# Paged decode attention: score tiles spread over eight 32x32 tiles, page turns moved further ahead, and the scores split round the values

## Chip, core and metric

The kernel runs on one core of one Trainium2 chip. The metric is the device time of one execution in microseconds (us): the median of three runs.

## What is computed

One inference step of a two-layer hybrid model, for a prompt of 1024 tokens and eight sample sequences of one new token each. The change touches one part alone: the attention of the eight new tokens of layer 0 over a paged cache of 8192 past positions (64 pages of 128 positions for each sequence). Everything is float32. Cut to what matters:

```python
past_ckv = cache_mla_ckv[li][page_table].reshape(n, -1, 256)      # n = 8 sequences, 8192 positions
past_kr  = cache_mla_krope[li][page_table].reshape(n, -1, 32)
q_lat  = einsum('nthd,chd->nthc', q_nope, w_uk)                   # 16 heads
s_past = (einsum('nthc,nlc->nhtl', q_lat, past_ckv) + einsum('nthr,nlr->nhtl', q_rope, past_kr)) * scale
p      = softmax(concat([s_past, s_new]))
o_lat  = einsum('nhtl,nlc->nthc', p[..., :l], past_ckv) + ...
```

## The kernel before, in words

The decode loop walks over 32 units (`WU`): eight sequences times four units of 16 pages (`UP`). A page is 128 positions x 288 numbers (256 latent and 32 rotary), 144 KB. For each unit w:

- **Fetch.** 16 DMAs bring the pages into one of three slots of `ck` (`CKS`), positions on partitions. For each of the four groups of four pages, SP issues two pages (`fetch_sp`, line 1176) and ACT issues the other two (`fetch_act`, line 1182). A slot may be refilled once the values of the unit that used it are done (`pv_done`). The issuing line is 1171.
- **Turn.** VectorE (DVE) transposes each group of four pages in 32x32 blocks from `ck` into one of two slots of `ckT` (`turn`, line 1308; the instruction is line 1311, 128x1152). In `ckT` the partition quarter b (partitions 32b to 32b+31, `quads[b]`) holds 32 columns of the cache for the positions of quarter b of each page.
- **Scores.** TensorE (PE) multiplies in 32x32 tiles (`scores`, line 1218; the instruction is line 1228). The nine steps j cover the 288 columns. In each step quarter b of `ckT` goes through the tile at row quarter b and column quarter b, so four tiles of the array's sixteen work at a time. One half of a unit is eight pages, that is 256 score columns. Both halves go into one PSUM bank, `x = w % 2`.
- **Softmax.** DVE takes the running maximum (`maximum`, line 1339: reduce at 1344, small copies across quarters to 1355), ACT takes the exponential (lines 1289 and 1291), DVE turns the probabilities (`turn_prob`, line 1357, instruction 1359), PE multiplies with the pages (`values`, line 1233, instruction 1241: all 128 rows, one column quarter for each page group) and DVE adds to the sums (`outputs`, line 1361, instructions 1366 and 1368).

Each engine has its instructions in an order written by hand, and they meet through semaphores. PE's order is: for each w, the second half of scores(w), the first half of scores(w+1), values(w). DVE's order for each w is: turn groups 0 and 1 of w+1, outputs(w-1), maximum(w), turn group 2 of w+1, turn_prob(w), turn group 3 of w+1. ACT's order for each w is: the exponentials of w, then the eight page issues of unit w+2. SP issues its pages one unit after another, waiting only for `pv_done`. While DVE does maximum(w), PE works on the first half of scores(w+1), whose groups 0 and 1 are turned already.

A float32 matmul stands in the trace as two records, so 72 matmuls of a unit's scores are 144 records, and the 16 of its values are 32.

Of the kernel before, what the change touches and what calls it, by code (L numbers as in the profile page):

```python
# [142 lines left out]
def build(nc, A, O):  # L143
    with ExitStack() as outer:
# [995 lines left out]
        with ExitStack() as ctx:  # L1140
# [38 lines left out]
                for g in range(4):  # L1179
                    fetch(sp, mybir.EngineType.SP, w, g, sp_pages)  # L1180

            def fetch_act(act, w):
                if w >= CKS:
                    act.wait_ge(pv_done, w - CKS + 1)
                for g in range(4):
                    fetch(act, mybir.EngineType.Activation, w, g, act_pages)

            with nc.Block() as block:
# [7 lines left out]
                @block.tensor  # L1196
                def _(pe):
                    MM = nc.tensor.matmul
                    pe.wait_ge(dec_w_in, 48)
                    for h in range(H):  # L1200
                        for c in range(2):
                            m = MM(bank[:, 6, (c * H + h) * NS:(c * H + h + 1) * NS], wukT[:, h, c * P:(c + 1) * P],
                                   qs[0:NOPE, h, :], start=True, stop=True)
                    m.then_inc(pe_i, 1)
                    pe.wait_ge(dve_i, 1)
                    for n in range(NS):
                        for half in range(2):

                            MM(bank[0:H, n // 2, (n % 2) * KVL + half * P:(n % 2) * KVL + (half + 1) * P],
                               cn[:, half, n, :], ident[:, :], start=True, stop=True)  # L1210
                            MM(bank[0:H, 7, n:n + 1], ql[:, half, n, :], z[:, 7 + half, T + n:T + n + 1],
                               start=half == 0, stop=False)
                        m = MM(bank[0:H, 7, n:n + 1], qr4[0:ROPE, n, :], z[0:ROPE, 9, T + n:T + n + 1],
                               start=False, stop=True)
                    m.then_inc(pe_i, 1)
                    pe.wait_ge(dve_i, 2)

                    def scores(w, half):

                        if w % NU == 0 and half == 0:  # L1220
                            pe.wait_ge(q_ready, w // NU + 1)
                        pe.wait_ge(turned, 2 * w + half + 1)
                        if w >= 2 and half == 0:
                            pe.wait_ge(p_done, w - 1)
                        x, pages = w % 2, slice(half * UP // 2, (half + 1) * UP // 2)
                        for j in range(NJ):
                            for b in range(4):
                                m = MM(bank[quads[b], x, half * 256:half * 256 + 256], qc[quads[b], (w // NU) % 2, j, :],  # L1228
                                       ckT[quads[b], x, pages, 32 * j:32 * j + 32], start=j == 0, stop=j == NJ - 1)
                        if half:  # L1230
                            m.then_inc(s_done, 1)

                    def values(w):
                        x = w % 2
                        pe.wait_ge(pt_done, w + 1)
                        if w >= 2:
                            pe.wait_ge(o_ev, w - 1)
                        for q in range(GP):
                            for g in range(4):
                                p = 4 * q + g  # L1240
                                m = MM(bank[quads[g], 2 + x, 0:KVL], probT[:, x, 32 * p:32 * p + 32],
                                       ck[:, w % CKS, p, 0:KVL], start=q == 0, stop=q == GP - 1)
                        m.then_inc(pv_done, 1)

                    scores(0, 0)
                    for w in range(WU):
                        scores(w, 1)
                        if w + 1 < WU:
                            scores(w + 1, 0)
                        values(w)  # L1250

                    pe.wait_ge(dve_i, 3)
                    nc.tensor.transpose(bank[0:NS, 7, 0:P], m_all[:, :], ident[:, :]).then_inc(pe_i, 1)
                    pe.wait_ge(dve_i, 4)
                    nc.tensor.transpose(bank[:, 5, 0:NS], top.rearrange("p a h -> p (a h)"), ident[0:NS, 0:NS]).then_inc(pe_i, 1)
                    pe.wait_ge(dve_i, 5)
                    MM(bank[:, 4, 0:NS * H], ones[:, :], lsel.rearrange("p n h -> p (n h)"), start=True, stop=True)
                    for n in range(NS):
                        for half in range(2):
                            m = MM(bank[:, 0, (half * NS + n) * H:(half * NS + n + 1) * H],  # L1260
                                   o_all[:, n, half * P:(half + 1) * P], sel[:, :], start=True, stop=True)
                    m.then_inc(pe_i, 1)
                    pe.wait_ge(dve_i, 6)
                    for h in range(H):
                        for c in range(2):
                            m = MM(bank[(h % 2) * DV:(h % 2 + 1) * DV, 1, (h // 2) * NS:(h // 2 + 1) * NS],
                                   wuv[:, c, h * DV:(h + 1) * DV], olat[:, c, :, h], start=c == 0, stop=c == 1)
                    m.then_inc(pe_i, 1)
# [3 lines left out]
                @block.scalar  # L1272
                def _(act):
                    act.wait_ge(pages_in, 16)
                    for w in range(CKS):
                        fetch_act(act, w)
                    act.wait_ge(dve_i, 1)
                    for b in range(2, 4):
                        for j in range(4):
                            m = nc.scalar.copy(by_block(qall[quads[b]])[:, :, :, j, :], ql[quads[j]])  # L1280
                    m.then_inc(q_copied, 1)
                    act.wait_ge(dve_i, 2)
                    for w in range(WU):
                        x, k = w % 2, slice(w % 2, w % 2 + 1)
                        act.wait_ge(mx_done, w + 1)
                        if w >= 2:
                            act.wait_ge(pt_done, w - 1)
                            act.wait_ge(o_ev, w - 1)
                        nc.scalar.activation(prob[:, x, :], bank[:, x, :], ACT.Exp, scale=MLA_SCALE, bias=nbias[:, k],
                                             accum_out=rs[:, k])  # L1290
                        nc.scalar.activation(decay[:, k], drop[:, k], ACT.Exp, scale=MLA_SCALE).then_inc(p_done, 1)
                        if w >= 1 and w + CKS - 1 < WU:
                            fetch_act(act, w + CKS - 1)
                    act.wait_ge(act_i, 1)
                    nc.scalar.activation(wts[:, :], wts[:, :], ACT.Exp, scale=MLA_SCALE).then_inc(act_i, 1)

                @block.vector
                def _(dve):
# [9 lines left out]
                    def turn(w, groups):  # L1308
                        for g in groups:
                            dve.wait_ge(page_in[(w % CKS) * 4 + g], (w // CKS + 1) * 16 * GP)  # L1310
                            m = V.transpose(ckT[:, w % 2, g * GP:(g + 1) * GP, :].rearrange("p a c -> p (a c)"),  # L1311
                                            ck[:, w % CKS, g * GP:(g + 1) * GP, :].rearrange("p a c -> p (a c)"))
                            if g % 2:
                                m.then_inc(turned, 1)

                    turn(0, (0, 1))
# [22 lines left out]
                    def maximum(w):  # L1339
# [1 line left out]
                        n, k = w // NU, slice(w % 2, w % 2 + 1)  # L1341
                        old = m_all[:, n:n + 1]
                        dve.wait_ge(s_done, w + 1)
                        ch.link(V.tensor_reduce(cmax[:, 0:1], bank[:, w % 2, :], AX, ALU.max))
                        for b in range(1, 4):
                            V.tensor_copy(cmax[0:32, b:b + 1], cmax[quads[b], 0:1])
                        ch.link(V.tensor_copy(cmax[0:32, 4:5], m_all[0:32, n:n + 1]))
# [8 lines left out]

                    def turn_prob(w):
                        dve.wait_ge(p_done, w + 1)
                        V.transpose(probT[:, w % 2, :], prob[:, w % 2, :]).then_inc(pt_done, 1)

                    def outputs(w):
                        n, k = w // NU, slice(w % 2, w % 2 + 1)
                        dve.wait_ge(pv_done, w + 1)
                        if w:
# [1 line left out]
                        V.scalar_tensor_tensor(out=l_all[:, n:n + 1], in0=l_all[:, n:n + 1], scalar=decay[:, k],  # L1366
                                               in1=rs[:, k], op0=ALU.mult, op1=ALU.add)
                        V.scalar_tensor_tensor(out=o_all[:, n, :], in0=o_all[:, n, :], scalar=decay[:, k],
                                               in1=bank[:, 2 + w % 2, 0:KVL], op0=ALU.mult, op1=ALU.add).then_inc(o_ev, 1)

                    queries(0)
                    for w in range(WU):
                        if (w + 1) % NU == 0 and w + 1 < WU:
                            queries((w + 1) // NU)
                        if w + 1 < WU:
                            turn(w + 1, (0, 1))
                        if w:
                            outputs(w - 1)
                        maximum(w)
                        if w + 1 < WU:  # L1380
                            turn(w + 1, (2,))
                        turn_prob(w)
                        if w + 1 < WU:
                            turn(w + 1, (3,))
                    outputs(WU - 1)

                    ch.link(V.tensor_copy(cmax[:, 0:1], mnew[:, :]))
# [855 lines left out]
```

## Time and profile before

| | us |
|---|---|
| median of three runs (3225.1 to 3228.49) | 3226.78 |
| the profiled execution's own time | 3227.78 |
| span of the profiled execution, first to last instruction | 3226.0 |
| mean granted TensorE clock over the span | 0.968 of full speed |

The profiled execution is 1.0 us above the median, and 1.78 us of its time lies outside the span. The decode loop is the stretch from about 776 to 1119 us of the span; before it stands the prompt's attention, after it the output projection. Times in the trace are in us from the start of the span. PE is TensorE's matmul, PEld its weight load, ACTq and SPq the sequencers that issue DMAs.

### The profile page before, as it was taken

The numbers are of one execution on the slowest core, as the hardware profiler recorded it, in microseconds if no ns is written. First come the engines' busy times: TensorE is split into PE (matmuls) and PEld (weight loads), VectorE is DVE, ScalarE is ACT, GpSimd is POOL, SyncE is SP. The second block draws the span as 40 slices with busy tenths as digits, with TensorE's granted clock in tenths as the row PEclk, the third lists the DMA queues.
The fourth block names the chain that finished last, engine by engine and source line by source line (L and its number), as shares of the span: only waits on it lengthen the run. The fifth ranks groups of instructions, "written<-read, shape, count | busy, mean of one in ns | idle before, by whom it ended". The sixth has DMA issues, their size and how long they took to land. (4 is left out here: it accounts for less than half of the span.)

```text
span 3226.0 us, 58525 instructions
## 1 busy us (share of the span) xinstructions
PE 3003.9 (93%) x23095; PEld 2627.9 (81%) x23095; DVE 1814.0 (56%) x2745; ACT 600.9 (19%) x1199; POOL 873.6 (27%) x496
## 2 busy tenths in 40 slices
PE   6967999998999889999999999997889999999996
PEld 6844666666555489999999999994589999999996
DVE  8795655565888645643524345667737515434354
ACT  3111444542000012110100001105512100000011
POOL 3300000100000045433434344420045344443432
PEclk9978999998999989999999999998989999999998
DMA  2100000003887521111111111202111111111112
GB/s 101 53 14 31 15 14 0 14 26 117 228 231 226 147 99 55 46 42 55 42 49 46 42 50 39 68 27 87 53 46 55 47 51 46 41 51 40 51 42 71
DMA packets 129158, 206.34 MB, mean 64 GB/s; under 512 B 14834, under 2 KB 95730, under 8 KB 128275
## 3 DMA queue, kind: packets, MB, share of 16 engines
q1 hardware_dynamic: 90994, 162.31, 16.4%
q10 hardware_dynamic: 38016, 41.99, 4.5%
q8 instruction: 102, 1.67, 0.2%
q14 instruction: 46, 0.37, 0.0%
HBM read 189.87 MB, written 6.25 MB: 61 GB/s over the span
## 5 line engine op out<-in xcount | busy, mean ns | idle before, releaser
L121 POOL TENSOR_TENSOR sb_slab_hi<-sb_slab_raw,sb_ones 128x1024 fp32r<-128x1024 f32 (+3 forms) x214 | 345.7, 1615 | 1725.2 <-PE ps_trunk_out L139 1053.0
L137 PE MATMUL ps_trunk_out<-sb_h_hi,sb_slab_hi 128*128 128x344 f32 x2400 | 768.0, 320 | 0.0
L138 PE MATMUL ps_trunk_out<-sb_h_hi,sb_slab_lo 128*128 128x344 f32 x2400 | 764.8, 319 | 0.0
L139 PE MATMUL ps_trunk_out<-sb_h_lo,sb_slab_hi 128*128 128x344 f32 x2400 | 764.4, 319 | 0.0
L123 POOL TENSOR_TENSOR sb_slab_lo<-sb_slab_raw,sb_slab_hi 128x1024 fp32r<-128x1024 f32 (+3 forms) x214 | 488.7, 2283 | 16.8
L138 PEld LDWEIGHTS ps_trunk_out<-sb_h_hi,sb_slab_lo 128*128 128x128 f32 x2400 | 450.4, 188 | 0.6
L137 PEld LDWEIGHTS ps_trunk_out<-sb_h_hi,sb_slab_hi 128*128 128x128 f32 x2400 | 450.4, 188 | 0.6
L139 PEld LDWEIGHTS ps_trunk_out<-sb_h_lo,sb_slab_hi 128*128 128x128 f32 x2400 | 450.4, 188 | 0.0
L137 PE MATMUL ps_trunk_out<-sb_ffn_a_hi,sb_slab_hi 128*128 128x344 f32 x1056 | 336.9, 319 | 4.9 <-DVEq L1529 4.9
L139 PE MATMUL ps_trunk_out<-sb_ffn_a_lo,sb_slab_hi 128*128 128x344 f32 x1056 | 337.9, 320 | 0.0
L138 PE MATMUL ps_trunk_out<-sb_ffn_a_hi,sb_slab_lo 128*128 128x344 f32 x1056 | 336.2, 318 | 0.0
L1228 PE MATMUL ps_dec_bank<-sb_dec_ckT,sb_dec_qc 32*32 32x256 f32 x4608 | 258.4, 378 | 4.8 <-DVEq L1332 3.6
L1228 PEld LDWEIGHTS ps_dec_bank<-sb_dec_ckT,sb_dec_qc 32*32 32x32 f32 x4608 | 142.8, 106 | 117.8 <-issue 17.2
L1482 ACT ACTIVATE sb_ffn_a<-sb_ffn_c 128x1032 f32<-128x1032 f32 x44 | 47.0, 1067 | 995.4 <-DVEq L1519 995.4
L1538 DVE TENSOR_TENSOR sb_z<-sb_z,ps_trunk_out 128x1032 f32 x48 | 59.0, 1230 | 300.5 <-PE ps_trunk_out L139 300.5
L137 PEld LDWEIGHTS ps_trunk_out<-sb_ffn_a_hi,sb_slab_hi 128*128 128x128 f32 x1056 | 198.4, 188 | 6.0 <-DVEq L1529 6.0
L139 PEld LDWEIGHTS ps_trunk_out<-sb_ffn_a_lo,sb_slab_hi 128*128 128x128 f32 x1056 | 198.5, 188 | 0.0
L138 PEld LDWEIGHTS ps_trunk_out<-sb_ffn_a_hi,sb_slab_lo 128*128 128x128 f32 x1056 | 198.4, 188 | 0.0
L930 POOL TENSOR_TENSOR sb_mla_diag<-sb_ident,sb_mla_rinv 128x256 f32<-128x256 f32 x64 | 39.2, 612 | 571.2 <-DVE sb_mla_rinv L1110 571.2
L1311 DVE STREAM_TRANSPOSE sb_dec_ckT<-sb_dec_ck 128x1152 f32<-128x1152 f32 x128 | 173.1, 1362 | 30.3 <-DMA sb_dec_ck<-cache 29.9
L1506 DVE TENSOR_TENSOR sb_ffn_g<-ps_trunk_out,sb_rstd 128x1032 f32<-128x1032 f32 x44 | 54.2, 1233 | 230.5 <-PE ps_trunk_out L139 230.5
L981 PE MATMUL ps_mla_bank<-sb_mla_k,sb_mla_q 96*128 96x512 f32 (+3 forms) x384 | 150.1, 502 | 1.8 <-ACT sb_mla_v L1041 1.8
(394 smaller groups left out, 4531.9 us busy)
## 6 DMA issues: line engine op xcount, KB each, us to landing
sb_slab_raw<-f_w_gu SPq DMA_DIRECT2D x88, 512.0 KB, 3.5
sb_dec_ck<-cache ACTq DMA_DIRECT2D x256, 144.0 KB, 2.8
sb_dec_ck<-cache SPq DMA_DIRECT2D x256, 144.0 KB, 3.1
sb_slab_raw<-f_w_down SPq DMA_DIRECT2D x32, 384.0 KB, 3.1
sb_slab_raw<-f_w_down SPq DMA_DIRECT2D x32, 320.0 KB, 2.9
sb_slab_raw<-e_w_out SPq DMA_DIRECT2D x24, 256.0 KB, 2.6
sb_slab_raw<-o_w_in SPq DMA_DIRECT2D x12, 512.0 KB, 3.5
sb_slab_raw<-e_w_in SPq DMA_DIRECT2D x10, 512.0 KB, 3.5
```

What stands on the lines that cost most here:

```text
L121: nc.gpsimd.tensor_tensor(hi, raw, one, ALU.mult).then_inc(self.hi_done[s], 1)
L123: nc.gpsimd.tensor_tensor(self.lo[:, s, 0:kc, :], raw, hi.bitcast(F32), ALU.subtract).then_inc(self.split_done[s], 1)
L137: nc.tensor.matmul(out[:, t, 0:TT], a, x_hi(k)[:, cols], start=k == 0, stop=False)
L138: nc.tensor.matmul(out[:, t, 0:TT], b, x_hi(k)[:, cols], start=False, stop=False)
L139: last = nc.tensor.matmul(out[:, t, 0:TT], a, x_lo(k)[:, cols], start=False, stop=k == kc - 1)
L930: nc.gpsimd.tensor_tensor(diag[:, big], ident[:, :].unsqueeze(1).broadcast_to((P, 2, P)), rinv[:, 2 * big:2 * big + 2].unsqueeze(2).broadc ...
L981: m = MM(score(u)[:, c0:c1], qg[:, h, qb * P:(qb + 1) * P], kg[:, h, c0:c1], start=True, stop=True)
L1228: m = MM(bank[quads[b], x, half * 256:half * 256 + 256], qc[quads[b], (w // NU) % 2, j, :], ckT[quads[b], x, pages, 32 * j:32 * j + 32], s ...
L1311: m = V.transpose(ckT[:, w % 2, g * GP:(g + 1) * GP, :].rearrange("p a c -> p (a c)"), ck[:, w % CKS, g * GP:(g + 1) * GP, :].rearrange("p ...
L1482: nc.scalar.activation(a[:, :], c[:, :], ACT.Gelu_apprx_tanh).then_inc(ffn_act_done, 1)
L1506: ch.link(V.tensor_tensor(v3(g[:, 2:]), slabs.out[:, 0, :, 0:TT], v3(rstd), ALU.mult))
L1538: V.tensor_tensor(xm, xm, slabs.out[:, s, :, 0:TT], ALU.add).then_inc(slabs.free[s], 1)
```

## The change

- Scores: the second half of a unit's pages is sent to the column quarter two further on, and to a bank of its own: half 0 of quarter b goes through the tile (row quarter b, column quarter b) into bank 2x, half 1 through the tile (row quarter b, column quarter b+2) into bank 2x+1. Both halves are in the same pass over j, so eight different tiles follow each other. The values go to banks 4 and 5.
- PE's order becomes, for each w: steps j = 0 to 3 of scores(w+1), values(w), steps j = 4 to 8 of scores(w+1). Scores of a unit need all four of its groups turned (`turned` counts units now).
- DVE's order becomes, for each w: maximum(w), turn group 3 of w+1, turn_prob(w), outputs(w-1), turn groups 0, 1 and 2 of w+2.
- turn_prob becomes three transposes: the first half of the probabilities as before, the second half with the partition halves exchanged.
- ACT's page issues: after the exponentials of w, the two pages of group 3 of w+2, then, after a wait for values(w), the six pages of groups 0 to 2 of w+3.
- The maximum and the exponential read two banks of 256 columns in place of one of 512.

```diff
-            def fetch_act(act, w):
+            def fetch_act(act, w, groups):
                 if w >= CKS:
                     act.wait_ge(pv_done, w - CKS + 1)
-                for g in range(4):
+                for g in groups:
                     fetch(act, mybir.EngineType.Activation, w, g, act_pages)
...
-                    def scores(w, half):
-
-                        if w % NU == 0 and half == 0:
-                            pe.wait_ge(q_ready, w // NU + 1)
-                        pe.wait_ge(turned, 2 * w + half + 1)
-                        if w >= 2 and half == 0:
-                            pe.wait_ge(p_done, w - 1)
-                        x, pages = w % 2, slice(half * UP // 2, (half + 1) * UP // 2)
-                        for j in range(NJ):
-                            for b in range(4):
-                                m = MM(bank[quads[b], x, half * 256:half * 256 + 256], qc[quads[b], (w // NU) % 2, j, :],
-                                       ckT[quads[b], x, pages, 32 * j:32 * j + 32], start=j == 0, stop=j == NJ - 1)
-                        if half:
+                    def scores(w, chunks):
+
+
+                        if chunks[0] == 0:
+                            if w % NU == 0:
+                                pe.wait_ge(q_ready, w // NU + 1)
+                            pe.wait_ge(turned, w + 1)
+                            if w >= 2:
+                                pe.wait_ge(p_done, w - 1)
+                        x = w % 2
+                        for j in chunks:
+                            for half in range(2):
+                                for b in range(4):
+                                    m = MM(bank[quads[(b + 2 * half) % 4], 2 * x + half, 0:256], qc[quads[b], (w // NU) % 2, j, :],
+                                           ckT[quads[b], x, half * UP // 2:(half + 1) * UP // 2, 32 * j:32 * j + 32],
+                                           start=j == 0, stop=j == NJ - 1)
+                        if chunks[-1] == NJ - 1:
                             m.then_inc(s_done, 1)
...
-                    scores(0, 0)
+                    scores(0, range(NJ))
                     for w in range(WU):
-                        scores(w, 1)
                         if w + 1 < WU:
-                            scores(w + 1, 0)
+                            scores(w + 1, range(4))
                         values(w)
+                        if w + 1 < WU:
+                            scores(w + 1, range(4, NJ))
...
-                            fetch_act(act, w + CKS - 1)
+                            fetch_act(act, w + CKS - 1, (3,))
+                        if w + CKS < WU:
+                            fetch_act(act, w + CKS, (0, 1, 2))
...
                     def turn_prob(w):
                         dve.wait_ge(p_done, w + 1)
-                        V.transpose(probT[:, w % 2, :], prob[:, w % 2, :]).then_inc(pt_done, 1)
+                        x, low, high = w % 2, slice(0, UP * 16), slice(UP * 16, UP * 32)
+                        V.transpose(probT[:, x, low], prob[:, x, low])
+                        V.transpose(probT[64:128, x, high], prob[0:64, x, high])
+                        V.transpose(probT[0:64, x, high], prob[64:128, x, high]).then_inc(pt_done, 1)
...
                     queries(0)
+                    turn(1, (0, 1, 2))
                     for w in range(WU):
                         if (w + 1) % NU == 0 and w + 1 < WU:
                             queries((w + 1) // NU)
+                        maximum(w)
                         if w + 1 < WU:
-                            turn(w + 1, (0, 1))
+                            turn(w + 1, (3,))
+                        turn_prob(w)
                         if w:
                             outputs(w - 1)
-                        maximum(w)
-                        if w + 1 < WU:
-                            turn(w + 1, (2,))
-                        turn_prob(w)
-                        if w + 1 < WU:
-                            turn(w + 1, (3,))
+                        if w + 2 < WU:
+                            turn(w + 2, (0, 1, 2))
                     outputs(WU - 1)
```

## Rows read from the trace of the kernel before

**Rows 1.** The page: its first line, and each engine's busy time.

```profile
span 3226.0 us, 58525 instructions
...
PE 3003.9 (93%) x23095; PEld 2627.9 (81%) x23095; DVE 1814.0 (56%) x2745; ACT 600.9 (19%) x1199; POOL 873.6 (27%) x496
```

**Rows 2.** Line 1344 alone: count, duration min/median/max in ns, first and last start.

```profile
L1344 DVE TENSOR_REDUCE sb_dec_cmax<-ps_dec_bank x32: 682/691/693, 786.7 to 1111.6; 128x1 f32<-128x512 f32 x32
```

**Rows 3.** Timeline of one unit: start us, us, engine, line, [idle before, releaser].

```profile
902.07 0.69 DVE L1344 TENSOR_REDUCE sb_dec_cmax<-ps_dec_bank 128x1 f32<-128x512 f32 x1 [1.49 <-PE ps_dec_bank L1228]
...
904.37 0.69 ACT L1289 ACTIVATE sb_z<-ps_dec_bank,sb_dec_nbias 128x512 f32<-128x512 f32 x1 [9.55 <-DVE sb_dec_nbias L1353]
904.45 1.37 DVE L1311 STREAM_TRANSPOSE sb_dec_ckT<-sb_dec_ck 128x1152 f32<-128x1152 f32 x1
...
905.51 5.03 ACTq L1171 DMA_DIRECT2D sb_dec_ck<-cache  x7
905.74 0.67 DVE L1359 STREAM_TRANSPOSE sb_z<-sb_z 128x512 f32<-128x512 f32 x1
906.34 1.33 DVE L1311 STREAM_TRANSPOSE sb_dec_ckT<-sb_dec_ck 128x1152 f32<-128x1152 f32 x1
...
906.47 1.93 PE L1241 MATMUL ps_dec_bank<-sb_dec_ck,sb_z 128*32 128x256 f32 x32 [0.58 <-DVE sb_z L1359]
...
908.33 7.97 PE L1228 MATMUL ps_dec_bank<-sb_dec_ckT,sb_dec_qc 32*32 32x256 f32 x144
...
911.48 0.47 DVE L1368 SCALAR_TENSOR_TENSOR sb_z<-sb_z,sb_dec_decay,ps_dec_bank 128x256 f32<-128x256 f32 x1
912.49 0.69 DVE L1344 TENSOR_REDUCE sb_dec_cmax<-ps_dec_bank 128x1 f32<-128x512 f32 x1 [0.53 <-PE ps_dec_bank L1228]
```

**Rows 4.** Timeline of PE alone at 279 us: column tiles with eight columns to stream.

```profile
278.90 0.25 PE L640 MATMUL ps_s_bank<-sb_s_hs,sb_s_c 128*32 128x8 f32 x8
278.99 0.23 PE L643 MATMUL ps_s_bank<-sb_s_nhi,sb_s_c 128*32 128x8 f32 x8
```

**Rows 5.** Timeline of PE alone at 206 us: row tiles, all 128 columns each.

```profile
206.03 1.47 PE L600 MATMUL ps_s_bank<-sb_mix,sb_s_wst 32*128 32x256 f32 x24
```

**Rows 6.** Timeline of PE alone: two bursts after idle, 205 to 260 us.

```profile
218.03 5.47 PE L624 MATMUL ps_s_bank<-sb_s_hh,sb_s_ca 128*32 128x256 f32 x64 [5.60 <-DVEq L810]
...
236.51 6.45 PE L624 MATMUL ps_s_bank<-sb_s_hh,sb_s_ca 128*32 128x256 f32 x64 [4.86 <-DVEq L810]
```

**Rows 7.** Timeline of PE alone: start and end of the decode loop.

```profile
775.99 14.56 PE L1228 MATMUL ps_dec_bank<-sb_dec_ckT,sb_dec_qc 32*32 32x256 f32 x216 [3.59 <-DVEq L1332]
...
1107.48 4.09 PE L1228 MATMUL ps_dec_bank<-sb_dec_ckT,sb_dec_qc 32*32 32x256 f32 x72
1115.61 3.30 PE L1241 MATMUL ps_dec_bank<-sb_dec_ck,sb_z 128*32 128x256 f32 x32 [4.04 <-DVE sb_z L1359]
```

**Rows 8.** Windows: stretch, length, busy (instructions) by engine, PEclk, DMA share, GB/s.

```profile
218.10:221.60 3.50, 3.50 (x36) 1.88 (x40) 3.50 (x5) 0.00 (x0) 0.00 (x0) 0.50 0.00 0
...
236.60:242.10 5.50, 5.50 (x56) 2.51 (x60) 5.50 (x6) 0.00 (x0) 0.00 (x0) 0.50 0.01 3
766.00:770.00 4.00, 4.00 (x37) 3.06 (x36) 1.89 (x2) 0.57 (x2) 0.00 (x0) 0.50 1.09 383
776.00:781.40 5.40, 5.40 (x52) 2.80 (x56) 2.42 (x2) 0.00 (x0) 0.00 (x0) 0.50 0.00 0
...
900.00:910.42 10.42, 9.84 (x184) 5.34 (x177) 7.54 (x20) 0.87 (x3) 0.00 (x0) 1.00 0.79 224
1107.50:1111.60 4.10, 4.07 (x76) 2.13 (x72) 0.61 (x2) 0.00 (x0) 0.00 (x0) 1.00 0.01 4
1111.60:1115.60 4.00, 0.00 (x0) 0.00 (x0) 2.94 (x13) 0.87 (x3) 0.00 (x0) 1.00 0.00 0
1116.10:1119.30 3.20, 2.81 (x28) 1.06 (x20) 0.35 (x2) 0.00 (x0) 0.00 (x0) 0.50 0.00 0
```

**Rows 9.** Line 1171, the page DMAs: issue to landing.

```profile
DMA to landing us min/median/max: 1.9/3.0/5.9
```

More of the change, by code:

```diff
@@ L1240, in values @@
                                 p = 4 * q + g
-                                m = MM(bank[quads[g], 2 + x, 0:KVL], probT[:, x, 32 * p:32 * p + 32],
+                                m = MM(bank[quads[g], 4 + x, 0:KVL], probT[:, x, 32 * p:32 * p + 32],
                                        ck[:, w % CKS, p, 0:KVL], start=q == 0, stop=q == GP - 1)
                         m.then_inc(pv_done, 1)
-                    scores(0, 0)
+                    scores(0, range(NJ))
                     for w in range(WU):
-                        scores(w, 1)
                         if w + 1 < WU:
-                            scores(w + 1, 0)
+                            scores(w + 1, range(4))
                         values(w)
+                        if w + 1 < WU:
+                            scores(w + 1, range(4, NJ))
                     pe.wait_ge(dve_i, 3)
@@ L1275, in _ @@
                     for w in range(CKS):
-                        fetch_act(act, w)
+                        fetch_act(act, w, range(4))
                     act.wait_ge(dve_i, 1)
@@ L1288, in _ @@
                             act.wait_ge(o_ev, w - 1)
-                        nc.scalar.activation(prob[:, x, :], bank[:, x, :], ACT.Exp, scale=MLA_SCALE, bias=nbias[:, k],
+                        nc.scalar.activation(prob[:, x, :].rearrange("p (a t) -> p a t", a=2), bank[:, 2 * x:2 * x + 2, 0:256], ACT.Exp, scale=MLA_SCALE, bias=nbias[:, k],
                                              accum_out=rs[:, k])
@@ L1312, in turn @@
                                             ck[:, w % CKS, g * GP:(g + 1) * GP, :].rearrange("p a c -> p (a c)"))
-                            if g % 2:
+                            if g == 3:
                                 m.then_inc(turned, 1)
@@ L1343, in maximum @@
                         dve.wait_ge(s_done, w + 1)
-                        ch.link(V.tensor_reduce(cmax[:, 0:1], bank[:, w % 2, :], AX, ALU.max))
+                        ch.link(V.tensor_reduce(cmax[:, 0:1], bank[:, 2 * (w % 2):2 * (w % 2) + 2, 0:256], mybir.AxisListType.XY, ALU.max))
                         for b in range(1, 4):
@@ L1368, in outputs @@
                         V.scalar_tensor_tensor(out=o_all[:, n, :], in0=o_all[:, n, :], scalar=decay[:, k],
-                                               in1=bank[:, 2 + w % 2, 0:KVL], op0=ALU.mult, op1=ALU.add).then_inc(o_ev, 1)
+                                               in1=bank[:, 4 + w % 2, 0:KVL], op0=ALU.mult, op1=ALU.add).then_inc(o_ev, 1)
                     queries(0)
+                    turn(1, (0, 1, 2))
                     for w in range(WU):
```

## The prediction

> **What bounds the kernel now.** I read the page first: PE is busy for 93% of the span [rows 1], so only a stage in which PE waits, or in which its array is part empty, has time to give. Then the line at which each unit of the decode loop begins its softmax: 32 starts from 786.7 to 1111.6, so 324.9/31 = 10.48 us for a unit [rows 2]. Then the timeline of one unit [rows 3], where the reader is to see a loop of two engines: the reduce at 902.07, DVE's chain to the probabilities, the values at 906.47, the second half of the next scores from 908.33, the next reduce at 912.49. PE is idle in it only 0.58 us before the values, because the first half of the next scores fills the time of DVE's chain. The clock of that unit, from 900 to 910.42, is full [rows 8]. So the decode loop is bound by PE, and PE by four tiles: 144 records take 7.97 us [rows 3] and 72 take 4.09 [rows 7], so 18 bursts of four take 3.88, 0.216 us each, and 0.21 is the last burst's tail.
>
> **Part 1, eight tiles at once.** The same 144 records are now 18 bursts of eight. Lower bound of a burst: 0.216, if all eight stream together. Upper bound: 0.432, if the second four wait for the first. Two rows lean to the lower. The values' four tiles share all 128 rows, and 32 records take 1.93 us [rows 3], four in each 0.216. Four row tiles that write all 128 columns do 24 records in 1.47 [rows 5], the same rate. So neither shared rows nor shared columns cost, and the change shares each two ways. Sequencing could be a floor: where little is streamed, 16 pairs of load and matmul start between 278.90 and 279.22 at the latest [rows 4], some 20 ns a pair; eight pairs in 0.216 need 27. I take 0.216: the scores of a unit fall from 7.8 to 3.9 us.
>
> The Trainium skill's page "TensorE: Matmul & The Clock Gate", Part 3 (packing small matmuls), says that a weight load runs beside matmuls in flight only when it goes to another row group. By that rule the second four would wait and a burst would cost 0.432. The trace does not agree where it can be seen: the values' loads go to all rows every time.
>
> **Part 2, the new order.** Before, PE had the first half of scores(w+1) to do during maximum(w). Now the scores of w+1 cannot start until group 3 of w+1 is turned, that turn stands behind maximum(w) on DVE, and maximum(w) waits for the last score of w. PE has nothing in between. The chain of a unit, from reduce to reduce, at full clock:
> - maximum 2.38 (902.07 to 904.45) and the turn of group 3, 1.37 [rows 3];
> - hand-over to PE 0.06 (906.41, the turned probabilities, to 906.47) [rows 3];
> - steps 0 to 3: 8 bursts, 1.73; change of tile shape 0.13 (values 906.47 to 908.33 is 1.86, 8 bursts are 1.73); values 1.86 [rows 3];
> - steps 4 to 8: 10 bursts, 2.16, tail 0.21, hand-over 0.06.
>
> Sum 9.96 us, against 10.48. PE's idle stretch is 0.06 + 2.38 + 1.37 + 0.06 = 3.87 us in every unit.
>
> **Part 3, DVE.** turn_prob: one transpose of 512 columns took 0.67, one of 1152 took 1.37 [rows 3], so 256 come to 0.39, some 0.35 back to back. Three: 1.05, with bounds 0.9 (three halves of the 0.60 between starts) and 2.0 (three full ones). It lies beside the first steps: probabilities are ready 3.75 + 1.05 = 4.8 us after the reduce begins, the values start at 5.7. DVE's sum is 2.38 + 1.30 + 1.05 + outputs 0.57 + three turns 3.9 = 9.2, under 9.96; only at the upper bound would DVE set the pace, by 0.2. The reduce and the exponential read as many elements from two banks as from one; I take them equal, at 0.69 each. Were each to pay 0.2 for the second bank, the reduce would add 0.2 to the chain and the exponential nothing.
>
> **Part 4, the page issues.** SP's order is as before, released at pv_done. ACT's eight issues are the same, moved: two after the exponentials, then a wait for values(w), then six. Behind that wait on ACT stands exp(w+1), and for that wait DVE's turn_prob and PE's values. Seven issues took 5.03 us [rows 3], 0.72 each. The values end 7.6 us after the reduce; six issues, begun about a microsecond later, end near 12.7, that is 2.7 into the next unit, where the exponential is due at 2.30 (904.37). It is 0.4 late, and the values have 0.9 in hand: nothing, by that cover. The pages themselves land in 3.0 us, at most 5.9 [rows 9]; they are needed about 7 us or more after their issue. The loop needs 2.36 MB in 9.96 us, 237 GB/s; 383 have been moved, from 766 to 770 [rows 8]. Nothing.
>
> **Part 5, the clock.** What the idle stretch does is the largest term. At the loop's end stands the same stretch once: scores end at 1111.57, the values start 4.04 us later [rows 7]. The clock was full before and during it, and 0.50 from 1116.1 to 1119.3 [rows 8]: the 32 records took 3.30 in place of 1.93 [rows 7, 3]. Two earlier bursts began after 5.60 and 4.86 us of idle [rows 6], and ran at 0.50 from 218.1 to 221.6 and from 236.6 to 242.1 [rows 8]. The loop's first scores began after 3.59 us [rows 7], with the clock low before as well, and were at 0.50 until 781.4 [rows 8]. So I expect that the level falls from 2.4 to 1.2 GHz round every unit's 3.87 us, and that the burst works at half rate for a while. The low stretches of work shown last 3.2, 3.6, 5.4 and 5.6 us; half is lost: 1.6 to 2.8 us a unit, mean 2.2. I take 2.0, since a fall can come after the burst has begun (3.30 is less than twice 1.93). The unit becomes 11.96 us.
>
> **Start and end.** The first scores need 18 bursts in place of 36, up to the reduce at 786.7: 5.5 us at half clock do 12.8 of them, the rest take 1.1, so the reduce comes near 782.9: -3.8 us. The last turn_prob is 0.4 longer and nothing covers it.
>
> **Sum.** 31 x (11.96 - 10.48) = +45.9, -3.8, +0.4: +42.5. The profiled execution took 3227.8, so 3270.3; the median stands 1.0 lower: 3269 us.
>
> **Rivals.**
> - *The clock stays full.* The idle stretch is a little shorter than those of [rows 6] and the 4.04, and a burst of 5.9 us follows each. If the level holds, the unit is 9.96: 31 x -0.52 - 3.4 = -19.5, 3207 us, faster. It decides whether the level survives this stretch. Against it: none of the stretches shown was survived. Chance 0.13.
> - *The clock falls in some units only*, half of them say: 10.96 a unit, +11.5, 3238 us; between 3226 and 3250 by the share. Chance 0.11.
> - *The change does not do what it says: the eight tiles go four by four*, the Trainium skill's rule above, as a mechanism: loads wait for matmuls in the same rows. Then steps 0 to 3 cost 3.46 and steps 4 to 8 4.32, the unit is 13.85 at full clock and 15.85 with the low stretch, and the start gains nothing: 3331 to 3394 us. Against it, [rows 3] and [rows 5]. A clock that stays low for the whole burst gives nearly the same, 15.8 a unit. Chance 0.07 for both.
>
> **How the numbers follow.** My forecast, the clock's fall in nearly every unit, has 0.69; its own range, from 1.6 and 2.8 lost a unit, is 3256 to 3293 us. The wider range reaches down to 3232, which takes in most of the second rival, and up to 3298 for the reduce's 0.2 a unit; the first and third rival, 0.20 together, are left out. A measurement here can tell about 0.2%, 6.5 us, from no change. Faster by more than that: the first rival and a little of the second, 0.14. Within it: 0.04, of the second. Slower: 0.82.
>
> **What would show it.** The reduce's 32 starts should span 31 x 12.0 us, and begin near 783. The scores' first record of each unit should have some 3.9 us of idle before it, released by DVE's turn. The granted clock over the loop should be well below full, near 0.8, with long and short units. A window at full clock should hold 18 bursts in 3.9 us. The exponential should sometimes wait for issues on ACT, and the values rarely for the probabilities. I am wrong if the loop's clock is full, or if eight records do not start together within 0.216 us.

## The result, and the profile after

The changed kernel takes 3272.23 us (median of four runs, 3268.99 to 3273.48), the kernel before 3227.6 in the same comparison: a ratio of 1.014, 95% interval 1.0125 to 1.0155. It is slower by some 45 us. The forecast was 3269, the range 3232 to 3298. The profiled execution took 3273.48 us.

The page of the changed kernel, its first lines and the granted clock in 40 slices of the span:

```profile
span 3271.7 us, 58589 instructions
## 1 busy us (share of the span) xinstructions
PE 2943.1 (90%) x23095; PEld 2585.3 (79%) x23095; DVE 1833.9 (56%) x2809; ACT 601.4 (18%) x1199; POOL 874.6 (27%) x496
...
PEclk9978999997777779999999999998989999999998
```

Against [rows 1] PE's share falls from 93% to 90% while the span grows, and the clock stands at 7 tenths in the slices that hold the decode loop. The line of the reduce, now 1351, gives the length of a unit (count, duration min/median/max in ns, first and last start):

```profile
L1351 DVE TENSOR_REDUCE sb_dec_cmax<-ps_dec_bank x32: 690/692/693, 784.2 to 1154.7; 128x1 f32<-128x512 f32 x32
```

That is (1154.7 - 784.2)/31 = 11.95 us, where [rows 2] give 10.48: 45.6 us over the 31 units, as much as the whole loss (a gain at the loop's start and a loss behind it cancel, see the sum below). The timeline of one unit of the changed kernel and the ends of its neighbours (start us, us, engine, line, [idle before, releaser]):

```profile
891.90 0.69 DVE L1351 TENSOR_REDUCE sb_dec_cmax<-ps_dec_bank 128x1 f32<-128x512 f32 x1 [2.86 <-PE ps_dec_bank L1231]
...
895.71 3.32 PE L1231 MATMUL ps_dec_bank<-sb_dec_ckT,sb_dec_qc 32*32 32x256 f32 x64 [3.91 <-DVE sb_dec_ckT L1318]
...
898.96 1.93 PE L1245 MATMUL ps_dec_bank<-sb_dec_ck,sb_z 128*32 128x256 f32 x32
900.83 2.39 PE L1231 MATMUL ps_dec_bank<-sb_dec_ckT,sb_dec_qc 32*32 32x256 f32 x80
903.32 0.69 DVE L1351 TENSOR_REDUCE sb_dec_cmax<-ps_dec_bank 128x1 f32<-128x512 f32 x1 [1.99 <-PE ps_dec_bank L1231]
...
905.70 1.37 DVE L1318 STREAM_TRANSPOSE sb_dec_ckT<-sb_dec_ck 128x1152 f32<-128x1152 f32 x1
906.26 0.69 ACT L1294 ACTIVATE sb_z<-ps_dec_bank,sb_dec_nbias 128x512 f32<-128x512 f32 x1 [11.11 <-DVE sb_dec_nbias L1360]
...
907.13 3.67 PE L1231 MATMUL ps_dec_bank<-sb_dec_ckT,sb_dec_qc 32*32 32x256 f32 x64 [3.92 <-DVE sb_dec_ckT L1318]
907.16 0.45 DVE L1367 STREAM_TRANSPOSE sb_z<-sb_z 128x256 f32<-128x256 f32 x1
...
910.73 2.64 PE L1245 MATMUL ps_dec_bank<-sb_dec_ck,sb_z 128*32 128x256 f32 x32
...
913.29 2.39 PE L1231 MATMUL ps_dec_bank<-sb_dec_ckT,sb_dec_qc 32*32 32x256 f32 x80
915.79 0.69 DVE L1351 TENSOR_REDUCE sb_dec_cmax<-ps_dec_bank 128x1 f32<-128x512 f32 x1 [2.63 <-PE ps_dec_bank L1231]
```

Read it against [rows 3]. The 0.58 us of idle before the values is gone; in its place stands 3.9 us before the first scores, in every unit. The waits from 785 to 1160 us (waiter, waited for, us, times, longest) put 24 of the 31 down to DVE's turn of group 3, the others to nothing that the profile shows:

```profile
PE ps_dec_bank L1231 <- DVE sb_dec_ckT L1318: 93.9, 24, 3.9
PE ps_dec_bank L1231 <- issue: 27.7, 7, 4.0
```

At full clock the last five steps of the scores, 80 records, take 2.39 us, ten bursts of eight. The first four steps, 64 records, would be 1.96 at that rate; here they take 3.32 and 3.67. So the eight tiles work as meant, and the time is lost in the bursts that follow the idle. The windows say why (stretch, length, busy by engine, PEclk, DMA share, GB/s); the first line is of the kernel before, the others of the changed one:

```profile
800.00:1110.00 310.00, 291.21 (x5204) 158.23 (x5200) 252.81 (x570) 25.53 (x90) 0.00 (x0) 1.00 0.77 220
...
800.00:1150.00 350.00, 236.17 (x5172) 120.86 (x5160) 268.83 (x627) 25.24 (x87) 0.00 (x0) 0.78 0.64 194
903.00:915.80 12.80, 8.77 (x184) 4.19 (x176) 9.47 (x24) 0.87 (x3) 0.00 (x0) 0.73 0.64 195
891.90:903.30 11.40, 7.50 (x176) 3.95 (x176) 9.14 (x21) 0.87 (x3) 0.00 (x0) 0.85 0.68 209
```

The mean clock of the loop is 0.78, against 1.00 before; the longer unit has the lower mean, 0.73 against 0.85.

### The profile page after: what moved, and what is told of

It is laid out like the page before. It is cut to its first block and busy times, and to the rows that moved or that the text cites. A ratio compares the mean times of both kernels' runs of the same rounds, so it can differ in the third digit from the quotient of the medians.

```text
span 3271.7 us, 58589 instructions
## 1 busy us (share of the span) xinstructions
PE 2943.1 (90%) x23095; PEld 2585.3 (79%) x23095; DVE 1833.9 (56%) x2809; ACT 601.4 (18%) x1199; POOL 874.6 (27%) x496
## 5 line engine op out<-in xcount | busy, mean ns | idle before, releaser
L1231 PE MATMUL ps_dec_bank<-sb_dec_ckT,sb_dec_qc 32*32 32x256 f32 x4608 | 188.0, 478 | 125.3 <-DVE sb_dec_ckT L1318 93.9
L1231 PEld LDWEIGHTS ps_dec_bank<-sb_dec_ckT,sb_dec_qc 32*32 32x32 f32 x4608 | 98.7, 130 | 204.7 <-DVE sb_dec_ckT L1318 105.5
```

Source lines behind the costliest of these rows:

```text
L1231: m = MM(bank[quads[(b + 2 * half) % 4], 2 * x + half, 0:256], qc[quads[b], (w // NU) % 2, j, :], ckT[quads[b], x, half * UP // 2:(half + ...
```

## The experiments

**e1: the idle stretch filled.** Dummy matmuls behind the last scores, with nobody waiting for them:

```diff
                         if w + 1 < WU:
                             scores(w + 1, range(4, NJ))
+                            for _ in range(14):
+                                MM(bank[:, 7, 0:P], ones[:, :], ident[:, :], start=True, stop=True)
```

> The changed kernel, with 14 dummy matmuls (128x128 ones times identity, into an unused bank) behind the last scores of each unit, where PE is idle. They take 14 x 0.215 = 3.0 us at full clock, less than the 3.9 us of idle, so they delay nothing by themselves. Theory (the idle stretch lowers TensorE's clock): the granted clock of the loop is full again, a unit falls from 11.95 to about 10.0 us, and the kernel from 3272 to about 3210 us, below the kernel before. Rival (the order of the chain, the late exponentials or the three transposes of the probabilities cost the time): a unit stays at 11.9 us or grows, 3270 us or more.

Measured: 3217.51 us, 0.997 of the kernel before (0.9958 to 0.9983). The clock of the loop, the reduce, and PE from the end of one unit to the end of the next:

```profile
800.00:1100.00 300.00, 282.50 (x6084) 200.65 (x6068) 268.70 (x627) 25.24 (x87) 0.00 (x0) 1.00 0.74 227
```

```profile
L1353 DVE TENSOR_REDUCE sb_dec_cmax<-ps_dec_bank x32: 691/692/693, 783.3 to 1100.4; 128x1 f32<-128x512 f32 x32
```

```profile
904.65 3.00 PE L1231 MATMUL ps_dec_bank<-sb_dec_ckT,sb_dec_qc 32*32 32x256 f32 x80
907.58 3.39 PE L1257 MATMUL ps_dec_bank<-sb_ident,sb_ones 128*128 128x128 f32 x28
911.50 1.96 PE L1231 MATMUL ps_dec_bank<-sb_dec_ckT,sb_dec_qc 32*32 32x256 f32 x64 [0.53 <-DVE sb_dec_ckT L1320]
913.39 1.93 PE L1245 MATMUL ps_dec_bank<-sb_dec_ck,sb_z 128*32 128x256 f32 x32
915.26 2.39 PE L1231 MATMUL ps_dec_bank<-sb_dec_ckT,sb_dec_qc 32*32 32x256 f32 x80
917.57 3.39 PE L1257 MATMUL ps_dec_bank<-sb_ident,sb_ones 128*128 128x128 f32 x28
```

Adding work to PE made the kernel 55 us faster than the changed one. The clock is at 1.00, the first four steps take 1.96, and from the dummies at 907.58 to those at 917.57 a unit is 9.99 us; from reduce to reduce 24 of the 31 units take 10.05 to 10.15, against 9.96 in the prediction's chain. This shows the clock to be the cause of the loss, and the order and the late exponentials not to be. The mean unit, 317.1/31 = 10.23, is a little longer, which is why the kernel comes to 3217 and not 3210: the first unit, ahead of which no dummies stand, takes 12.45 us with the clock at 0.50 from 785.4 to 792 us, and in six others the last 80 records take 2.62 to 3.25 us in place of 2.39, as at 904.65. Why those six do, no run shows.

**e2: a part of it filled.** The same with 5 in place of 14.

> The same with 5 dummy matmuls, 1.1 us of the idle stretch: about 2.8 us stay idle. Theory: the clock falls in some units and not in others, a unit between 10.0 and 11.95 us, about 10.8, the kernel between 3210 and 3272 us, about 3236. If any matmul at all in the stretch is enough, as e1; if only a filled stretch is enough, 3272 us.

Measured: 3227.11 us, 1.0005 of the kernel before (0.9995 to 1.0014).

```profile
800.00:1105.00 305.00, 228.38 (x5423) 142.59 (x5415) 267.10 (x623) 25.21 (x87) 0.00 (x0) 0.96 0.73 222
```

```profile
L1353 DVE TENSOR_REDUCE sb_dec_cmax<-ps_dec_bank x32: 684/692/693, 783.3 to 1110.1; 128x1 f32<-128x512 f32 x32
```

Two of its units on PE:

```profile
904.53 3.53 PE L1231 MATMUL ps_dec_bank<-sb_dec_ckT,sb_dec_qc 32*32 32x256 f32 x64 [2.65 <-issue]
...
912.17 1.38 PE L1257 MATMUL ps_dec_bank<-sb_ident,sb_ones 128*128 128x128 f32 x10
916.15 1.96 PE L1231 MATMUL ps_dec_bank<-sb_dec_ckT,sb_dec_qc 32*32 32x256 f32 x64 [2.60 <-DVE sb_dec_ckT L1320]
```

A mean clock of 0.96 and a unit of 326.8/31 = 10.54: between the two, nearer to full clock. With 2.6 us left idle the clock falls in some units and not in others, as expected: the scores at 904.53 pay, those at 916.15 do not. The middle of the range expected was 0.3 us a unit too high.

**e3: four tiles in the new order.** This undoes the spreading, and with it the three transposes of the probabilities that it needs:

```diff
-                                    m = MM(bank[quads[(b + 2 * half) % 4], 2 * x + half, 0:256], ...
+                                    m = MM(bank[quads[b], 2 * x + half, 0:256], ...
...
-                        V.transpose(probT[:, x, low], prob[:, x, low])
-                        V.transpose(probT[64:128, x, high], prob[0:64, x, high])
-                        V.transpose(probT[0:64, x, high], prob[64:128, x, high]).then_inc(pt_done, 1)
+                        V.transpose(probT[:, w % 2, :], prob[:, w % 2, :]).then_inc(pt_done, 1)
```

> The changed order, but both halves of a unit go through the four tiles on the diagonal (half 1 in a bank of its own still), and turn_prob is one transpose again. Theory (eight tiles stream together, and the new order needs it): 18 more bursts of 0.216 us a unit, 3.9 us: a unit of 13.9 us if the clock holds and 15.8 with the same low stretch, 3335 to 3397 us. Rival (the second four tiles add nothing): no slower than the changed kernel, 3272 us.

Measured: 3379.32 us, 1.0472 (1.0454 to 1.0489), inside the range expected. A unit on PE:

```profile
1006.92 4.99 PE L1231 MATMUL ps_dec_bank<-sb_dec_ckT,sb_dec_qc 32*32 32x256 f32 x64 [3.87 <-DVE sb_dec_ckT L1318]
1011.84 1.93 PE L1245 MATMUL ps_dec_bank<-sb_dec_ck,sb_z 128*32 128x256 f32 x32
1013.70 4.52 PE L1231 MATMUL ps_dec_bank<-sb_dec_ckT,sb_dec_qc 32*32 32x256 f32 x80
```

At full clock (1.00 from 1013.7 to 1018.2 us) 80 records take 4.52 us where eight tiles take 2.39. The spreading is worth 3379 - 3272 = 107 us in this order, with the clock low in part of both loops, and the order without it loses 152 against the kernel before.

**e4: group 3 turned with its unit.** DVE's order is changed so that the turn leaves the chain:

```diff
-                    turn(1, (0, 1, 2))
+                    turn(1, (0, 1, 2, 3))
...
                         maximum(w)
-                        if w + 1 < WU:
-                            turn(w + 1, (3,))
+                        if w + 2 < WU:
+                            turn(w + 2, (0,))
                         turn_prob(w)
                         if w:
                             outputs(w - 1)
                         if w + 2 < WU:
-                            turn(w + 2, (0, 1, 2))
+                            turn(w + 2, (1, 2, 3))
```

> Group 3 of unit w+1 is turned with the others of its unit, ahead of maximum(w), and group 0 of w+2 takes its place behind maximum(w); scores of w+1 can then begin while DVE works on the maximum of w. Theory: the idle stretch of 3.9 us splits, the largest part left is some 2.9 us before the values. If the clock holds, DVE sets the unit with 9.2 to 9.4 us, 3190 us; if it falls in some units, up to 11 us a unit, 3243. Rival (the time lies in the length of PE's and DVE's work, not in who waits for whom): as the changed kernel, 3272 us.

Measured: 3257.57 us, 1.0089 (1.0073 to 1.0106): above the range expected and below the rival's 3272. The step of the expectation that failed is the size of the idle left, 3.4 to 4.1 us in the two units on PE shown and not 2.9:

```profile
913.33 3.35 PE L1245 MATMUL ps_dec_bank<-sb_dec_ck,sb_z 128*32 128x256 f32 x32 [3.44 <-DVE sb_z L1369]
916.61 4.32 PE L1231 MATMUL ps_dec_bank<-sb_dec_ckT,sb_dec_qc 32*32 32x256 f32 x144
925.03 1.51 PE L1245 MATMUL ps_dec_bank<-sb_dec_ck,sb_z 128*32 128x256 f32 x12 [4.10 <-DVE sb_z L1369]
```

```profile
800.00:1140.00 340.00, 234.82 (x5164) 121.28 (x5164) 267.12 (x622) 25.21 (x87) 0.00 (x0) 0.79 0.65 197
```

The idle has only moved from before the scores to before the values; the values now pay (3.35 us for 32 records), and the clock is 0.79, nearly as low as in the changed kernel.

**e5: the kernel before, with a stretch of idle.** Four tiles, old turns, old issues:

```diff
                         scores(w, 1)
+                        values(w)
                         if w + 1 < WU:
                             scores(w + 1, 0)
-                        values(w)
```

> The kernel before, with one thing changed: the first half of scores(w+1) stands behind values(w) on PE, not ahead of it, so PE has nothing to do from the last score to the probabilities, some 4.4 us in each unit. Four tiles, four-way order, page issues and turns as before. At full clock a unit is 4.4 + 1.9 + 8.2 = 14.5 us, 3352 us in all. Theory (an idle stretch of this length lowers the clock, whatever the tiles): some 2 us more in each unit, 16.5 us, 3414 us, and a granted clock well below full in the loop. Rival (the fall belongs to the eight tiles or to the new order): 3352 us at full clock.

Measured: 3430.22 us, 1.0627 (1.0609 to 1.0645). One unit on PE, and the clock of the loop:

```profile
1010.37 3.64 PE L1241 MATMUL ps_dec_bank<-sb_dec_ck,sb_z 128*32 128x256 f32 x32 [4.47 <-DVE sb_z L1359]
1013.94 9.02 PE L1228 MATMUL ps_dec_bank<-sb_dec_ckT,sb_dec_qc 32*32 32x256 f32 x144
1027.43 3.64 PE L1241 MATMUL ps_dec_bank<-sb_dec_ck,sb_z 128*32 128x256 f32 x32 [4.48 <-DVE sb_z L1359]
```

```profile
800.00:1310.00 510.00, 375.75 (x5268) 174.21 (x5264) 256.37 (x582) 26.12 (x90) 0.00 (x0) 0.80 0.48 135
```

A unit is 1027.43 - 1010.37 = 17.06 us where the full-clock sum is 14.5: 2.6 lost, 0.6 more than the theory's 2. The values take 3.64 against 1.93 and the 144 records of the scores 9.02 against 7.97 [rows 3]. So the fall needs neither eight tiles nor the new turns; a stretch of idle in every unit brings it without them.

**e6: ACT's page issues put back**, in e1:

```diff
-                            fetch_act(act, w + CKS - 1, (3,))
-                        if w + CKS < WU:
-                            fetch_act(act, w + CKS, (0, 1, 2))
+                            fetch_act(act, w + CKS - 1, range(4))
```

> e1 (14 dummy matmuls), with ACT's page issues where they stood in the kernel before: all four groups of w+2 behind the exponentials of w. Theory (the turns of groups 0 to 2, now ahead, need the pages that much earlier): their issues run from 3.4 to about 9 us after the reduce and land 3 us later, the turns want the first at 5.6, so DVE waits for DMAs and a unit grows from 10.2 to 11 to 12 us, 3241 to 3272 us. Rival (the pages come early enough either way, the late exponentials cost more): 3217 us or less.

Measured: 3253.91 us, 1.0084 (1.0067 to 1.0101), inside the range expected and 36 us over e1. The two longest waits from 785 to 1100 us:

```profile
ACT sb_z L1296 <- DVE sb_dec_nbias L1360: 300.2, 28, 12.3
DVE sb_dec_ckT L1318 <- DMA sb_dec_ck<-cache: 40.9, 48, 2.2
```

DVE waits 40.9 us for pages; no such wait is among e1's. Where DVE waits, PE comes to wait too, and some of the 36 us goes by way of the clock, which is 0.96 from 785 to 1130 us. With the idle filled, the earlier issues are a needed part of the change.

**e7 and e8: the scores divided at step 7**, on top of e4 (`range(7)` and `range(7, NJ)` in place of `range(4)` and `range(4, NJ)`); e8 also divides ACT's issues two groups and two groups.

> e4 with the scores divided at step 7 in place of step 4. In e4 PE idles 3.4 us between its first scores and the values and the clock still falls; seven steps (3.0 us) in front leave 2.1 us there, and some 1.3 us behind the last two steps. Theory: the clock holds in nearly all units, DVE sets the unit at 9.4 to 9.6 us, 3191 to 3198 us. Rival (what is left of idle is still enough for a fall): as e4, 11 us or more, 3243 us or more.

> e7 with ACT's issues divided evenly: groups 2 and 3 of w+2 behind the exponentials of w, groups 0 and 1 of w+3 behind values(w), so that fewer issues stand ahead of the next exponentials. Theory: the exponentials are on time; 0 to 0.5 us a unit against e7, 3180 to 3198 us. Rival (pages of groups 0 to 2 come later and DVE waits for them): up to 3210 us.

Measured: e7 3211.32 us, 0.9947 (0.993 to 0.9964); e8 3215.51 us, 0.9964 (0.9949 to 0.9978). The clock of e7's loop, and two of its idle stretches before the values:

```profile
785.00:1090.00 305.00, 209.44 (x5320) 114.17 (x5309) 279.44 (x652) 27.01 (x93) 0.00 (x0) 0.92 0.75 227
```

```profile
811.23 3.64 PE L1245 MATMUL ps_dec_bank<-sb_dec_ck,sb_z 128*32 128x256 f32 x32 [3.96 <-DVE sb_z L1369]
...
1002.88 1.93 PE L1245 MATMUL ps_dec_bank<-sb_dec_ck,sb_z 128*32 128x256 f32 x32 [1.61 <-DVE sb_z L1369]
```

And DVE's waits for pages, in e7 (785 to 1100 us) and in e8 (785 to 1095 us):

```profile
DVE sb_dec_ckT L1318 <- DMA sb_dec_ck<-cache: 11.6, 24, 2.1
...
DVE sb_dec_ckT L1318 <- DMA sb_dec_ck<-cache: 23.3, 31, 1.8
```

With no dummy work, the division alone takes the clock from e4's 0.79 to 0.92 and 46 us off. It does not reach the 3191 to 3198 expected: the clock does not hold in nearly all units. Where exponentials come late, up to 3.8 us after their reduce in place of 2.3, the idle before the values grows, as at 811.23, and the values pay. e8 does what its theory wanted, every exponential begins 2.3 to 2.4 us after its reduce; but DVE's waits for pages double, as its rival had it, and it is 4 us slower than e7, above both ranges expected.

**e9 and e10: the same two orders with the idle filled**, 6 and 3 dummies at division 7 (e9), 12 and 3 at division 4 (e10).

> e7 with 6 dummy matmuls between the seven steps and the values (1.3 of some 1.7 us idle) and 3 behind the last two steps (0.6 us). In e7 the clock of the loop was still at half for 51 us and units lay between 9.35 and 12.7 us, 10.0 in the mean; the shortest are DVE's own sum. Theory: with the idle filled the clock stays full, a unit is 9.4 to 9.6 us, 3192 to 3199 us. Rival (what keeps e7 above 9.4 is the pages or the late exponentials): as e7, 3209 to 3214 us.

> e4 (division at step 4, group 3 turned ahead) with 12 dummy matmuls before the values and 3 behind the scores. e4 took 3257 us with 147 us of the loop at half clock. Theory: full clock, DVE sets the unit at 9.4 to 9.6 us, 3192 to 3200 us, as e9, since the place of the division matters through the clock alone. Rival (the division itself costs): well above e9.

Measured: e9 3210.96 us, 0.995 (0.9937 to 0.9964); e10 3210.94 us, 0.9955 (0.9941 to 0.9968). e9 lies in the range of its rival, and e10 is not above e9. The loop of e10, its clock and its two longest waits from 785 to 1100 us:

```profile
785.00:1090.00 305.00, 297.88 (x6227) 211.94 (x6235) 277.37 (x644) 26.09 (x90) 0.00 (x0) 1.00 0.75 228
```

```profile
ACT sb_z L1298 <- DVE sb_dec_nbias L1364: 284.7, 31, 11.0
DVE sb_dec_ckT L1322 <- DMA sb_dec_ck<-cache: 13.2, 23, 1.9
```

```profile
L1355 DVE TENSOR_REDUCE sb_dec_cmax<-ps_dec_bank x32: 651/684/692, 780.5 to 1092.2; 128x1 f32<-128x512 f32 x32
```

e10 against e4 is 47 us for dummy matmuls alone: the division mattered through the clock. But both missed what was expected: at full clock a unit of e10 is still 311.7/31 = 10.06. The rows say where it goes: DVE is busy for 277.37 of the 305.00 us, 9.15 us a unit, and its only long wait is for pages, 13.2 us or 0.4 a unit; most of the rest are short gaps between its own instructions. So with the clock out of the way DVE and the pages bound the loop, by this trace; no run shows it by taking those waits away. It also explains why e9's dummies bring nothing that e7 has not: in e7, at a clock of 0.92, DVE is already busy for 279.44 of its 305.00 us. All of e7, e9 and e10 beat both kernels, by 0.5% against the kernel before; e7 does it without any dummy work.

## Why the prediction was right, step by step

- **Part 1, eight tiles.** Right: 80 records in 2.39 us are ten bursts of 0.216 and the tail, the lower bound. By the Trainium skill's rule on weight loads and row groups ("TensorE: Matmul & The Clock Gate", Part 3) they would have taken about 4.5 us, an estimate from ten bursts of 0.432 and the tail. The trace does not agree with the rule for tiles of different column quarters; 4.52 us is what e3's four tiles take.
- **Part 2, the chain.** Right: 3.91 and 3.92 us of idle against 3.87, and with the clock held (e1) 10.06 us for most units against 9.96; the mean of e1, 10.23, has a few longer units in it, for which the chain has no term.
- **Part 3, DVE.** Within the bounds, a little dearer than taken: the transposes of lines 1367 to 1369 have medians of 0.40, 0.44 and 0.44 us, 1.28 together, against 1.05 taken and bounds of 0.9 and 2.0. That makes DVE's sum 9.4, still under the chain. The reduce takes 692 ns from two banks, 691 from one [rows 2]: nothing, as taken.
- **Part 4, the issues.** The cover held: the exponential at 906.26 is 2.94 us after its reduce in place of 2.30, 0.6 late and not 0.4, and others of the loop are up to 1.3 late, but the only wait of the values for the probabilities is the one at the loop's end. That the issues had to move is e6.
- **Part 5, the clock.** Right in kind and size: 11.95 against 11.96 us. e1 (filled, gone), e2 (partly filled, most of it gone) and e5 (made in the kernel before) show the cause. The 2.0 us a unit was a choice near the middle of four rows. Measured against e1's 10.06 the mean loss is 1.89, made of two: in the short units the first scores pay alone (3.32 for 1.96), 1.4 us, in the long ones the values pay too (3.67 for 1.96 and 2.64 for 1.93), 2.4 us. That the mean fell so near to 2.0 is luck, and so is part of the unit's closeness: the chain was 0.1 short where the loss was 0.1 long.
- **Start and end.** The first reduce came at 784.2 where 782.9 was said, because this execution's loop began later, at 777.63 and not 775.99 (why, no row shows): from the first score to the reduce it is 6.6 against 6.9 us, where before it was 10.7.
- **The sum.** Predicted +42.5 for the profiled execution, 3270.3; it took 3273.48, +45.7. The units gave 45.6 where 45.9 was said, the first reduce -2.5 for -3.8, and the time from the last reduce to the end +2.6 for +0.4. Of that last term 0.6 is the longer turn of the last probabilities and 0.3 the last values, 3.64 us in place of 3.30; the rest no row here shows.

## What to carry to other kernels

When an order is changed so that one engine does its work faster but in one piece, price the idle that opens beside it, and ask of TensorE what its clock does after an idle stretch of that length elsewhere in the same trace. Here a gain of 0.5 us a unit by the sum (0.25 in e1's mean unit) became 1.5 us of loss. Dividing the work so that the idle falls in shorter parts took 46 us off (e7 against e4); where that cannot be done, matmuls that nobody needs can stand in the stretch (e1), and a profile of that run tests whether the clock is the cause. Then look for the next bound: here DVE was busy for nine tenths of the loop once the clock held (e10), and more dummies had nothing to win.

## What the runs showed of the hardware that was not expected

Units of the changed kernel alternate with great regularity between two lengths, as 11.42 and 12.47 us in the first timeline above (reduces at 891.90, 903.32 and 915.79), with mean clocks of 0.85 and 0.73; long and short units had been expected, but not this regularity. In e5, by contrast, the unit settles at 17.06 us, with the values wholly at half rate each time (3.64 us) and part of the scores. And the price is not linear in the idle: e2's five dummies are busy for 1.38 us of the stretch, which leaves 2.6 us of idle out of 3.9, and most of the loss is gone (10.54 us a unit, between 11.95 unfilled and 10.23 filled). Stretches of nearly the same length, 2.65 and 2.60 us, are followed by slow scores in one unit and by scores at full rate in another (904.53 and 916.15 in e2).
